# Down products of a gated feed-forward: activations in two buffers of their own, the next weights requested in pieces

## The reference, cut to what matters

```python
def conv_ffn(x, w_up, conv_w, conv_b, w_down):
    h = x @ w_up                       # (2048, 1024) @ (1024, 2 x 2816)
    h = depthwise_causal_conv(h, conv_w) + conv_b     # width 3
    val, gate = jnp.split(h, 2, axis=-1)
    return (jax.nn.gelu(gate) * val) @ w_down         # the down product, (2048, 2816) @ (2816, 1024)

h = h + conv_ffn(rms_norm(h, norm_ffn_g[i]), ...)
gate = jax.nn.sigmoid(rms_norm(h, norm_ple_g[i]) @ ple_w_gate[i])     # the last stage
h = h + gate * (p[i] @ ple_w_proj[i])
```

## Time and profile before

| | us |
|---|---|
| median of 3 runs | 2889.82 (2889.08 to 2893.59) |
| the profiled execution, its own time | 2886.86 |
| its span, from first to last instruction | 2885.3 |
| PE busy in the span | 2607.5 (90%) |
| DVE, ACT, POOL busy | 1712.4, 1368.2, 509.6 |
| mean granted TensorE clock | 0.955 |
| down products of half 0 | 1659.03 to 1923.29 |
| down products of half 1 | 2344.99 to 2604.95 |

### The profile page before, as it was taken

The page is one execution under the profiler, slowest core; times in us unless marked ns, Lnnn a source line. Parts: engine busy times, 40 slices in busy tenths (PEclk is TensorE's granted clock), DMA queues, the critical chain, the costliest instruction groups (busy, mean ns, idle before and its releaser), DMA issues. The chain is left out here.

```text
span 2885.3 us, 38789 instructions
## 1 busy us (share of the span) xinstructions
PE 2607.5 (90%) x13883; PEld 2239.3 (78%) x13883; DVE 1712.4 (59%) x3358; ACT 1368.2 (47%) x2460; POOL 509.6 (18%) x309
## 2 busy tenths in 40 slices
PE   6999997999845799489999999999999998997998
PEld 5989986999834588478888777778888876775876
DVE  1110272777596776488888755578888864444333
ACT  3343332666423666455555444455555542334444
POOL 3454454666300121000000000000000000000000
PEclk9999998999977799789999999999999999998999
DMA  4665456888333253312222366642222246662221
GB/s 163 195 213 172 152 170 157 188 185 185 70 100 126 87 182 129 104 59 88 88 81 75 116 208 232 224 146 88 88 81 75 87 152 245 223 205 99 79 76 46
DMA packets 313909, 392.09 MB, mean 136 GB/s; under 512 B 22161, under 2 KB 222161, under 8 KB 310650
## 3 DMA queue, kind: packets, MB, share of 16 engines
q1 hardware_dynamic: 299850, 341.60, 39.2%
q0 software_dynamic: 13888, 48.25, 4.3%
HBM read 298.59 MB, written 95.33 MB: 137 GB/s over the span
## 5 line engine op out<-in xcount | busy, mean ns | idle before, releaser
L2355 PE MATMUL ffn_bank<-ffn_x,ffn_ring 128*128 128x512 f32 x880 | 346.0, 393 | 19.1 <-DVE ffn_ring L2149 13.6
L2356 PE MATMUL ffn_bank<-ffn_x,ffn_ring 128*128 128x512 f32 x880 | 345.4, 393 | 0.0
L2357 PE MATMUL ffn_bank<-ffn_x,ffn_ring 128*128 128x512 f32 x880 | 345.4, 392 | 0.0
L504 ACT ACTIVATE att_exps<-att_scores,att_part 128x256 f32<-128x256 f32 (+1 forms) x384 | 153.1, 454 | 124.4 <-DVE att_part L475 121.7
L2355 PEld LDWEIGHTS ffn_bank<-ffn_x,ffn_ring 128*128 128x128 f32 x880 | 166.8, 190 | 55.8 <-DVE ffn_ring L2149 9.1
L475 DVE CUSTOM_DVE_ANT_0 att_scores<-att_bank,att_bias 128x256 f32<-128x256 f32 (+1 forms) x384 | 122.5, 363 | 141.3 <-PE att_bank L422 66.1
L2422 POOL DMA_DIRECT2D ffn_act<-ffn_late x88 | 47.6, 541 | 858.7 <-DVE ffn_late L2201 858.7
L2188 DVE SCALAR_TENSOR_TENSOR ffn_strips<-ffn_strips,ffn_taps 128x512 f32<-128x512 f32 x176 | 132.0, 750 | 111.9 <-ACT ffn_strips L1999 111.9
L938 POOL TENSOR_TENSOR in_w_lo<-in_w,in_w_hi 128x2048 fp32r<-128x2048 f32 x36 | 166.0, 4612 | 183.3 <-ACT in_w_hi L821 183.3
L2357 PEld LDWEIGHTS ffn_bank<-ffn_x,ffn_ring 128*128 128x128 f32 x880 | 166.8, 190 | 34.9
L2356 PEld LDWEIGHTS ffn_bank<-ffn_x,ffn_ring 128*128 128x128 f32 x880 | 166.9, 190 | 34.5
(11 more groups left out here) (337 smaller groups left out, 7004.0 us busy)
## 6 DMA issues: line engine op xcount, KB each, us to landing
ffn_w<-in_ffn_w_up SPq DMA_DIRECT2D x88, 512.0 KB, 4.7
ffn_w<-in_ffn_w_down SPq DMA_DIRECT2D x40, 1024.0 KB, 7.1
in_w<-in_w_in SPq DMA_DIRECT2D x36, 1024.0 KB, 6.2
ffn_act<-ffn_late POOLq DMA_DIRECT2D x88, 256.0 KB, 2.7
ffn_sums<-ffn_act SPq DMA_DIRECT2D x88, 256.0 KB, 4.5
ffn_strips<-ffn_act SPq DMA_DIRECT2D x88, 256.0 KB, 4.5
mixed_part<-branch_results SPq DMA_DIRECT2D x16, 792.0 KB, 5.3
z_rows<-in_result SPq DMA_DIRECT2D x80, 128.0 KB, 2.5
```

Of the source, the lines that this page charges most:

```text
L504: nc.scalar.activation(exps[:, n % RING, m * width:(m + 1) * width], scores[:, n % RING, m * width:(m + 1) * width], ACT.Exp, bias=part[:, ...
L2355: pe.matmul(out[:, :], hi[:, k], x_hi[kind][:, k], start=(k == 0 and fresh), stop=False, skip_group_check=not fresh)
L2356: pe.matmul(out[:, :], hi[:, k], x_lo[kind][:, k], start=False, stop=False, skip_group_check=not fresh)
L2357: mm = pe.matmul(out[:, :], lo[:, k], x_hi[kind][:, k], start=False, stop=(k == KH - 1), skip_group_check=not fresh)
```

## The change

- Raw activations get two buffers of their own, `a_raw[0]` and `a_raw[1]` (`RAW` = 2), apart from the ring; the rows of taps, used earlier, are laid over that memory. SyncE's `load_a` now waits only for VectorE's split of the feature two before (`a_lo_ready`), and loads run two ahead instead of four.
- The wait for the ring slot moves from SyncE's `load_a` into ScalarE's `split_a`.
- `AHEAD` is 3 instead of 2: ScalarE and VectorE do, for each unit j, the split of unit j+1, then the splits of features 4j+3 to 4j+6. Ahead of the first down unit they split features 0 to 2 instead of 0 to 3.
- The eight gate loads are issued one at a time, each after the activation loads of a unit: units 0, 1, 3, 4, 5 of pass 1 and 0, 1, 3 of pass 2.

```diff
-    AHEAD = 2
+    AHEAD = 3
     RING = 4
+    RAW = 2
...
-        tap_rows = st.sb("tap_rows", [2 * F, N_TAPS, P])
+        a_raw = [st.sb(f"a_raw{r}", [P, BANK]) for r in range(RAW)]
+        tap_rows = st.over("tap_rows", [2 * F, N_TAPS, P], F32, nc.sbuf_base - RAW * BANK * 4)
...
-        a_exact = [sums[:, 1], sums[:, 3], plain[:, BANK:2 * BANK], plain[:, 3 * BANK:4 * BANK]]
...
-        a_loaded = st.sems("a_loaded", RING)
+        a_loaded = st.sems("a_loaded", RAW)
...
             def load_a(a):
...
-                r = a % RING
-                if a >= h * PASSES * F + RING:
-                    wait_feature_done(sp, *divmod(a - RING, F))
-                elif r < 2:
-                    sp.wait_ge(w_lo_ready, operand_count(h, at[h][F - 1, 7]))
-                else:
-                    sp.wait_ge(conv_ready, (h * F + F - 1) * 4)
+                if a >= RAW:
+                    sp.wait_ge(a_lo_ready, a - RAW + 1)
                 sp.wait_ge(act_stored[o % RING], (o // RING + 1) * DMA)
...
-                sp.dma_start(a_exact[r], act_rows[f][:, col:col + BANK]).then_inc(a_loaded[r], DMA)
+                sp.dma_start(a_raw[a % RAW][:, :], act_rows[f][:, col:col + BANK]).then_inc(a_loaded[a % RAW], DMA)
...
-                for a in range(first, first + RING):
+                for a in range(first, first + RAW):
                     load_a(a)
                 for p in range(PASSES):
...
-                    if h + 1 == HALVES and p == 1:
-                        sp.wait_ge(product_done, HALVES * N)
-                        for part, src, loaded in w_gate_loads:
-                            sp.dma_start(part, src).then_inc(loaded, DMA)
                     for j, fs in enumerate(unit_features):
                         load_w_after(h * UNITS + F + p * PER_PASS + j)
                         for f in fs:
-                            a = (h * PASSES + p) * F + f + RING
+                            a = (h * PASSES + p) * F + f + RAW
                             if a < last_of_half(h):
                                 load_a(a)
...
+                        if h + 1 == HALVES and p in (1, 2) and j != 2 and p * PER_PASS + j < 2 * PER_PASS + 4:
+                            n = (p - 1) * (PER_PASS - 1) + j - (j > 2)
+                            part, src, loaded = w_gate_loads[n]
+                            if n == 0:
+                                sp.wait_ge(product_done, HALVES * N)
+                            sp.dma_start(part, src).then_inc(loaded, DMA)
...
             def split_a(a):
-                r = a % RING
-                act.wait_ge(a_loaded[r], (a // RING + 1) * DMA)
-                nc.scalar.copy(a_hi[r], a_exact[r]).then_inc(a_hi_ready, 1)
+                h, p, f = feature(a)
+                act.wait_ge(a_loaded[a % RAW], (a // RAW + 1) * DMA)
+                if a >= h * PASSES * F + RING:
+                    wait_feature_done(act, *divmod(a - RING, F))
+                elif a % RING < 2:
+                    act.wait_ge(w_lo_ready, operand_count(h, at[h][F - 1, 7]))
+                else:
+                    act.wait_ge(conv_ready, (h * F + F - 1) * 4)
+                nc.scalar.copy(a_hi[a % RING], a_raw[a % RAW][:, :]).then_inc(a_hi_ready, 1)
...
                     if j == N - 1:
-                        for a in range(first, first + RING):
+                        for a in range(first, first + AHEAD):
                             split_a(a)
...
                             a = (h * PASSES + p) * F + f + AHEAD
-                            if first + RING <= a < last_of_half(h):
+                            if a < last_of_half(h):
                                 split_a(a)
```

More of the change, by code:

```diff
@@ L2162, in split_a @@
                 dve.wait_ge(a_hi_ready, a + 1)
-                nc.vector.tensor_tensor(a_lo[r], a_exact[r], a_hi[r].bitcast(F32), ALU.subtract).then_inc(a_lo_ready, 1)
+                nc.vector.tensor_tensor(a_lo[r], a_raw[a % RAW][:, :], a_hi[r].bitcast(F32), ALU.subtract).then_inc(a_lo_ready, 1)
             def add(h, f, kind):
```

## The result

The changed kernel takes 3015.74 us (median, 3014.4 to 3020.02); the kernel before took 2891.06 us beside it. The ratio is 1.0437 (95% interval 1.0423 to 1.0452): slower by about 125 us. The forecast was +97 us, 2987, in a range up to 3015. The time lies 0.7 us above that range.

A forecast was written before the change was run, and what follows sets the result against it. TensorE, busy nearly throughout the down stretches, would give way to a closed loop of 13.2 us a turn against 10.9 of matmuls. Half 0 gains 45.8 us, half 1 51.5, together 97: forecast 2987 us, range 2925 to 3015.

The forecast's parts named there:

- The closed loop: Down stretches: weights, activation load, copies and splits wait on each other; a full turn takes 13.2 us against 10.9 of matmuls.
- ScalarE's idle time: Sign of being right: in the down stretches, ScalarE's idle time ended by activation loads is far above before.
- the third and fourth feature of a unit: Where TensorE would stall in each down unit: about 1.0 us before the third, 1.3 us before the fourth.
- the first feature of a pass: At each pass's start, TensorE waits about 4.4 us: weights' split ends 12.6 us after E, with 8.2 us of work.
- the way between the halves: Up products between the two down stretches: no term in the sum, which covers only the two halves.
- Gate pieces inside the loop: Half 1: seven of eight gate loads stand between a load and the weights, taken at 1.0 us each.
- Half 0: First down stretch: four row loads of 512 KB ahead of one turn's weights add 5.2 us; total 310.1, 45.8 more.
- the next half's normalisation, transposes and first operands: Half 0: normalisation of next rows and transposes fall into the loop's load wait, costed at nothing.
- A: Weights land as with nothing in flight, 5.7 for 7.43 us: +40 us, 2930; chance 0.13, including times up to the forecast.
- B: Activation load not held by weights ahead, landing in about 3 us: turn 9.4 us, kernel -22, 2868; chance 0.05.
- C: TensorE's clock falls lastingly to half after waits: a unit takes 21.8 us, up to 479 us added, 3365; chance 0.02.
- D: Nothing happens overall: gate stall goes, loop costs about as much, needing a turn near 11 us and cheap starts; chance 0.03.

## Why the prediction was wrong

**The mechanism was right.** The closed loop with a turn of 13.2 us is there, at 13.5 in the turn shown and 13.2 in the one before it; ScalarE's idle time ends with activation loads; most of TensorE's waits stand at the third and fourth feature of a unit; the first feature of a pass waits 4.3 us on average and 5.1 at most, through the weights' split. The loop alone, half 1 without gate loads, took 309.9 us where the prediction's own sum without its 7 us of pieces is 304.5. Opening the loop on either side gave back 78 and 92 us. Half 1 with no gate loads in either kernel grew by 64.0 us (309.9 against 245.9), and 17.2 of these stay with two ahead; the loop proper is the larger part, not all of it.

**The step that failed is the sum of the sizes.** The terms beside the loop were too low or missing: the gate pieces, half 0's own work, and above all the way between the halves, which was put at nothing without a reason (+8.8 us). The loop's own sum was too low as well, by 5.4 us in half 1, where it can be read alone. From the windows, the 31.5 us between the sum of 97.3 and the 128.8 measured are: half 0 12.7, half 1 11.3, between the halves 8.8, 1.2 because half 0's time before was taken with the wait at its end, and less 2.5 at the start. The loop itself has 5.4 us of half 1's (309.9 against 304.5): the three whole passes take 78.9, 77.2 and 77.4 us from weight split to weight split instead of 76.6, 3.7 in all; the last three features take 9.9 instead of 8.2, the start 14.5 instead of 14, and the last turns are half a microsecond shorter than summed. For half 0 I assume the same 5.4.

*Gate pieces inside the loop*: "0.55 us (issue alone) to 1.29 each, I take 1.0". Measured 1.8 each: 12.9 us instead of 7. The upper bound was itself too low. It came from eight pieces that run into one another, 1.29 us apart, with nothing behind them that a loop waits for. In the loop a piece also holds up the weights and the load behind, and the first held that load up by 2.7 us.

*Half 0.* One group of four row loads was counted at 5.2 us. In the kernel with the gate loads last, the first pass of half 0 is 4.4 us longer than that of half 1 (86.7 and 82.3 us), which fits that size. But line 1836 issues four such loads a second time, ahead of the third pass, and the prediction left them out; that pass is 2.8 us longer than its fellow in half 1 (80.1 and 77.3). Both passes also carry squares and scaling of the next rows, so the loads' part in the 4.4 and 2.8 is argued and not shown. And what was costed at nothing, the next half's normalisation, transposes and first operands, was not covered wholly: the last pass with its end is 3.3 us longer (76.1 and 72.8). Its single parts were not tried apart. With the loop's 5.4 these make 10.7 of the 12.7 us; the rest is within what the same code varies by (320.2 and 322.8 us in two kernels).

*Between the halves* no cost was given. The first up product waits for VectorE's split of its operand. By the order of the code that stands behind the splits of half 0's last features, which now come late; no run parts this from other causes. Timeline, TensorE: the first up product after half 0, now, and in the kernel before.

```profile
1985.32 0.79 PE L2359 MATMUL ffn_bank<-tail_shared,ffn_ring 128*128 128x512 f32 x1 [5.81 <-DVE ffn_ring L2153]
1985.91 0.63 PE L2360 MATMUL ffn_bank<-tail_shared,ffn_ring 128*128 128x512 f32 x1
...
1990.87 0.40 PE L2360 MATMUL ffn_bank<-ffn_x,ffn_ring 128*128 128x512 f32 x1
```
```profile
1923.29 0.51 PE L2355 MATMUL ffn_bank<-tail_shared,ffn_ring 128*128 128x512 f32 x1 [1.03 <-DVE ffn_ring L2149]
```

4.8 us more of waiting, and twelve matmuls at half clock behind it (granted clock 0.50 from 1985.3 to 1990.6; each starts 0.43 us after the last instead of 0.24), 2.3 us; the last 1.7 us of the 8.8 I did not place. With two ahead 4.6 us of the 8.8 stay.

**The rivals.** *A*, weights landing as with nothing in flight: in the first pass of half 1 they took 6.1 to 7.2 us, in the whole half 5.0 to 8.5 with a median of 7.5, and the copy of the load behind started 7.5 to 7.7 us after their issue in the two turns read; false. The copy at 5.59 us appeared only with half the bytes. By an estimate from the fit in the Trainium skill, DMA: Bandwidth & Descriptors, section Anatomy of one DMA, 1 MB would land in 4.4 us. The page gives the fit for transfers that GpSimd requests; the prediction used it for SyncE's. The trace agrees with neither: 6.1 us at least in that first pass, with SyncE requesting, and 9.5 us (median of 36) with GpSimd requesting, both with other transfers in flight. *B*, the load not held: false, by the same rows. *C*, the clock: spells at half clock come behind the waits and the granted clock is 0.94 in both stretches, where it was 0.99 and 0.97. TensorE's busy time grew by some 20 us a half, but inside the halves the loop sets the pace, so that most of this replaces idle time. No lasting fall came. *D*: false; the gate stall went, but the loop costs far more.

**The range** ended at 3015 because all the bounds that it took in were of terms in the sum. Terms costed at nothing (half 0's cover, the way between the halves) had no upper bound, and they and the second group of row loads made about 15 us (3.3, 8.8 and 2.8).

## What to carry to other kernels

When a buffer's release moves from the consumer (TensorE) to an intermediate split, follow program order on every queue and look for a closed loop: if one turn, with a transfer's full latency in it, sums to more than the busiest engine's work, the loop sets the pace and every engine waits. Such a loop can be opened by the order on either side (what the copy engine takes first, or what the queue requests first), and here opening it on both sides gained 5.5 us over one. Opening it does not make the buffers enough: some 32 us stayed here. Requests that cost little while loads run well ahead (some 5 us for eight pieces here) cost more once loads are just in time (12 to 13), and each group of them must be counted from the code, in every pass. A residual is to be measured against a kernel without the same stall: against the kernel before, half 1's own stall hid what the buffers cost.

## What was not expected of the hardware

A load of 256 KB requested on SyncE after 1 MB of weights requested on GpSimd's queue reached its copy 8.90 us after the weights' request in the turn read, no sooner than behind them on one queue (7.73 us); the weights themselves landed later when GpSimd requested them (median 9.5 us for 1 MB instead of 6.9). With 512 KB ahead of it in place of 1 MB it did so after 5.59 us: 2.1 us for 512 KB less, while a gate piece of the same size, landing in a row of eight, took 1.29 us. What makes the difference was not tried.
